# Each head's columns of the compressed keys and values projected once, and the exchanged copy written by VectorE

## The reference, cut to what matters

```
k_c, v_c = columns of u @ w_in            # (256 tokens, 2 groups x 64) each
chunks = t.reshape(b, g, seq // 16, 16, 64)
blocks = concat([chunks[:, :, m:m + 15] for m in range(2)], axis=3) + pos_emb
flat   = blocks.reshape(b, g, 15, 32 * 64)
return gelu(flat @ w1 + b1) @ w2 + b2
```

## Time and profile before

| | |
|---|---|
| median of 3 runs | 1196.41 us (1195.58 to 1196.82) |
| the profiled execution | 1196.96 us, of which the span in the trace is 1194.9 us |
| PE busy | 1084.8 us, 91% of the span |
| DVE, ACT, POOL busy | 472.8, 412.7, 194.1 us |
| moved by DMA | 333.58 MB |

### The profile page before, as it was taken

The page is one execution under the profiler, slowest core; times in us unless marked ns, Lnnn a source line. Parts: engine busy times, 40 slices in busy tenths (PEclk is TensorE's granted clock), DMA queues, the critical chain, the costliest instruction groups (busy, mean ns, idle before and its releaser), DMA issues. The chain is left out here.

```text
span 1194.9 us, 17411 instructions
## 1 busy us (share of the span) xinstructions
PE 1084.8 (91%) x6862; PEld 706.2 (59%) x6862; DVE 472.8 (40%) x1046; ACT 412.7 (35%) x790; POOL 194.1 (16%) x272
## 2 busy tenths in 40 slices
PE   8999888999888988788888899878999899999997
PEld 7887545567422424344544235346887686999775
DVE  4566456435200001123333011106747546444655
ACT  5445453342110001104332002004436454444873
POOL 1002552000000000003120000004432223001550
PEclk9999999999999999999999999999999999999999
DMA  9657599826799999999999999995531203666300
GB/s 363 235 171 262 217 345 311 311 97 281 307 429 427 422 423 411 430 397 416 419 427 422 422 422 415 425 418 189 180 127 54 89 28 117 226 184 187 107 20 35
DMA packets 55720, 333.58 MB, mean 279 GB/s; under 512 B 5840, under 2 KB 6096, under 8 KB 43216
## 3 DMA queue, kind: packets, MB, share of 16 engines
q1 hardware_dynamic: 55632, 332.39, 71.6%
HBM read 331.32 MB, written 1.05 MB: 278 GB/s over the span
## 5 line engine op out<-in xcount | busy, mean ns | idle before, releaser
L486 ACT ACTIVATE ab<-w 128x1024 fp32r<-128x1024 f32 (+2 forms) x117 | 122.0, 1049 | 174.9 <-PE ps L502 171.1
L496 DVE TENSOR_TENSOR ab<-w,ab 128x1024 fp32r<-128x1024 f32 (+2 forms) x101 | 123.6, 1229 | 131.4 <-ACT ab L486 130.9
L2577 PE MATMUL ps<-w,vT 128*32 128x512 f32 x1024 | 126.6, 617 | 44.3 <-DMA w<-in_w_gate 28.5
L502 PE MATMUL ps<-ab,uA 128*128 128x512 f32 x320 | 101.3, 398 | 3.1 <-ACT gr L1591 1.3
L2577 PEld LDWEIGHTS ps<-w,vT 128*32 128x32 f32 x1024 | 28.7, 110 | 124.1 <-issue 76.0
L502 PE MATMUL ps<-UA,ab 128*128 128x256 f32 x512 | 93.8, 284 | 2.8 <-ACT h L1591 1.5
L502 PE MATMUL ps<-ab,UA 128*128 128x512 f32 (+1 forms) x288 | 87.9, 386 | 0.0
L502 PEld LDWEIGHTS ps<-UA,ab 128*128 128x128 f32 x512 | 80.2, 192 | 3.5 <-issue 1.7
L2625 PE MATMUL ps<-w,bT 128*32 128x512 f32 x512 | 63.0, 617 | 15.3 <-DMA w<-in_w_down 9.8
L502 PE MATMUL ps<-UB,ab 128*128 128x256 f32 x256 | 72.4, 283 | 0.0
L502 PEld LDWEIGHTS ps<-ab,uA 128*128 128x128 f32 x320 | 59.8, 190 | 17.8 <-issue 3.8
(11 more groups left out here) (554 smaller groups left out, 1883.4 us busy)
## 6 DMA issues: line engine op xcount, KB each, us to landing
w<-in_w_gate SPq DMA_DIRECT2D x32, 2048.0 KB, 13.4
w<-in_w_up SPq DMA_DIRECT2D x32, 2048.0 KB, 13.1
w<-in_w_down SPq DMA_DIRECT2D x32, 2048.0 KB, 13.4
w<-in_w_ada SPq DMA_DIRECT2D x48, 512.0 KB, 7.8
w<-in_w_c SPq DMA_DIRECT2D x42, 512.0 KB, 4.5
w<-in_w_m SPq DMA_DIRECT2D x16, 512.0 KB, 6.0
w<-in_ab_out_w SPq DMA_DIRECT2D x10, 512.0 KB, 4.7
w<-in_w_out SPq DMA_DIRECT2D x8, 512.0 KB, 9.4
```

The lines of the kernel that those rows point to most:

```text
L486: e.activation(sp.a(j), w.v, ACT.Copy).then_inc(sp.whole, 1)
L496: e.tensor_tensor(sp.b(j), w.v, sp.a(j).bitcast(F32), ALU.subtract).then_inc(sp.parts[j % NAB], 1)
L502: ins = e.matmul(out_, l[x], r[y], start=start and n == 0, stop=stop and n == 2)
L2577: ins = e.matmul(t.ps[o, :], ve[:, p % 2, 2 * c + k, o], w.v[:, 2 * a + k, :], start=c + k == 0, stop=c + k == 4)
```

## The change

The array `w_kvc` has 256 columns in place of 512: keys of group 0 and 1, values of group 0 and 1, each once. Its two tiles (kvc.0 and kvc.1) hold four of the eight contraction steps each, where four tiles held two. PE fills two banks, one for keys and one for values, with group 0 on partitions 0 to 63 and group 1 on 64 to 127. For each bank DVE now writes three pieces into `bS`: the bank as it is, its lower half into the upper partitions of a second place, and its upper half into the lower partitions. Then it makes all eight additions, reading from the first place where group and parity agree with the partitions, and from the second where they don't.

```diff
-        for n in ("gqk", "gv", "q", "kv", "kvc", "gr", "cq", "kva", "qa", "za", "zb"):
+        for n in ("gqk", "gv", "q", "kv", "gr", "cq", "kva", "qa", "za", "zb"):
...
+            if c < 2:
+                source[f"kvc.{c}"] = d["w_kvc"][:, 4 * c:4 * c + 4, :]
...
-            pe_linT(e, S1, "kvc", uA, uB)
+            two = [bank.take(ALL, "kvc") for _ in range(2)]
+            for c in range(2):
+                j = S1.add(f"kvc.{c}")
+                a, b = S1.a(j), S1.b(j)
+                S1.ready(e, j)
+                for m, t in enumerate(two):
+                    if c == 0:
+                        free(e, t)
+                    for k in range(4):
+                        o, n = slice(m * 128, m * 128 + 128), 4 * c + k
+                        ins = three(e, t.ps[:, 0:256], (a[:, k, o], b[:, k, o]), (uA[:, n, :], uB[:, n, :]), n == 0, n == 7)
...
-            act_lin(e, S1, "kvc", [])
+            act_splits(e, S1, "kvc.1", 3)
...
-            dve_lin(e, S1, "kvc")
+            rest_splits(e, "dve", S1, "kvc.1", 3)
             e.wait_ge(cleared, 1)
-            for j, t in enumerate(bank["kvc"]):
-                m, g = j // 2, j % 2
+            for m, t in enumerate(bank["kvc"]):
...
-                e.tensor_tensor(bS[:, 0, 0:256], t.ps[:, 0:256], rsrow[:, :], ALU.mult).then_inc(t.evac, 1)
+                e.tensor_tensor(bS[:, 0, 0:256], t.ps[:, 0:256], rsrow[:, :], ALU.mult)
+                e.tensor_tensor(bS[64:128, 1, 0:256], t.ps[0:64, 0:256], rsrow[0:64, :], ALU.mult)
+                e.tensor_tensor(bS[0:64, 1, 0:256], t.ps[64:128, 0:256], rsrow[64:128, :], ALU.mult).then_inc(t.evac, 1)
...
+                for g in range(2):
+                    for jp in range(2):
+                        p0 = 64 * jp
+                        src = bS[p0:p0 + 64, g ^ jp, 0:256].rearrange("p (n s) -> p s n", s=16)
...
-                if j < 3:
+                if m == 0:
                     V_.did(ins)
+                    rest_splits(e, "dve", S1, "gr.3")
...
-        "w_kvc": tiles(w_in, 8, *[half(col[m], g) for m in (1, 2) for g in (0, 0, 1, 1)]),
+        "w_kvc": tiles(w_in, 8, *[half(col[m], g) for m in (1, 2) for g in range(2)]),
```

More of the change, by code:

```diff
@@ L1457, in pe_first @@
             pe_lin(e, S1, "kv", uA, uB, 512, range(2))
-            pe_linT(e, S1, "kvc", uA, uB)
+            two = [bank.take(ALL, "kvc") for _ in range(2)]
[9 more added lines that the diff above has]
+                        ins = three(e, t.ps[:, 0:256], (a[:, k, o], b[:, k, o]), (uA[:, n, :], uB[:, n, :]), n == 0, n == 7)
+                    if c == 1:
+                        ins.then_inc(t.full, 1)
+                if c == 0:
+                    S1.gone(j, ins)
+                else:
+                    S1.done[j] = (t.full, t.n)
             pe_lin(e, S1, "gr", uA, uB, 512, range(2))
@@ L1784, in dve_first @@
                 V_.after()
-                e.tensor_tensor(bS[:, 0, 0:256], t.ps[:, 0:256], rsrow[:, :], ALU.mult).then_inc(t.evac, 1)
+                e.tensor_tensor(bS[:, 0, 0:256], t.ps[:, 0:256], rsrow[:, :], ALU.mult)
+                e.tensor_tensor(bS[64:128, 1, 0:256], t.ps[0:64, 0:256], rsrow[0:64, :], ALU.mult)
+                e.tensor_tensor(bS[0:64, 1, 0:256], t.ps[64:128, 0:256], rsrow[64:128, :], ALU.mult).then_inc(t.evac, 1)
                 e.wait_ge(t.evac, t.n)
[L1787 to L1792, removed]
-                if j < 3:
+                for g in range(2):
+                    for jp in range(2):
+                        p0 = 64 * jp
+                        src = bS[p0:p0 + 64, g ^ jp, 0:256].rearrange("p (n s) -> p s n", s=16)
+                        for half in range(2):
+                            ins = e.tensor_tensor(Bt[p0:p0 + 64, m, 8 * half:8 * half + 8, 15 * g:15 * g + 15], src[:, jp:16:2, half:half + 15],
+                                                  bc(pos[p0:p0 + 64, 8 * half:8 * half + 8], 2, 15), ALU.add)
+                if m == 0:
                     V_.did(ins)
+                    rest_splits(e, "dve", S1, "gr.3")
                 else:
                     ins.then_inc(cmp_rows, 1)
-                if j == 1:
-                    rest_splits(e, "dve", S1, "gr.3")
             dve_lin(e, S1, "gr")
```

## The result

| | before | after |
|---|---|---|
| median of the runs, us | 1196.58 (1194.3 to 1197.9) | 1190.43 (1186.85 to 1192.48) |
| profiled execution, us | 1196.96 | 1191.98 |
| its span, us | 1194.9 | 1190.2 |
| PE busy, us | 1084.8 | 1079.1 |
| granted clock, mean | 0.986 | 0.986 |

The ratio is 0.9948, with a 95% interval of [0.9929, 0.9967]: 6.2 us, between 3.9 and 8.5. The forecast was 1189.1, range 1187.3 to 1192.3. The time is right to 1.3 us, and the way to it is half right. The experiments show that the gain is that of the removed matmuls. Of the 1.5 us that the sum adds to them, 1.3 rest on a fall of the clock that one execution of the kernel before had and another had not.

A forecast was written before the change was run, and what follows sets the result against it. The prediction took PE to bound the projections and transfers the experts. Its terms, 5.76 + 1.87 - 0.32 = 7.3 us, gave a forecast of 1189.1 us, with 1187.3 to 1192.3 for 8 in 10.

The forecast's parts named there:

- What it removes on PE: In kvc, 48 matmuls of 256 columns in place of 96, at 120 ns each: 5.76 us less.
- What it adds on DVE: For the kvc banks, 0.42 us per exchanging piece, 3.90 us a bank; DVE 0.57 us later against gr's start.
- m00.0 and m00.3: At m00: start 12.7 us after gr's start (T), last quarter waiting 0.7 us for DVE's split; gain against T 1.87 us.
- The clock: In m00: no clock fall expected behind a pause cut from 1.34 to 0.58 us; m00 took 12.72 us, gr 11.0.
- Rival 1: Behind la, the clock falls all the same and m00 takes its 12.72 us: gain 6.5 us, 1189.9; chance 0.17.
- m10.2: At m10.2, PE waits 0.3 us for POOL's split, leaving 1.5 us of gain against gr's start.
- Does it reach the end?: From 130 us on, the experts included, the same timeline 7.3 us earlier, since DMA queues are almost empty there.
- the turned banks: In the first GLA product, the second half no longer shares bank 4 with an unread result: at most 0.3 us, left out.
- the sign of being wrong: Late gr.3 (pause at 75 us), exchanging piece over 0.7 us, or shift of 7 us at 130 and less at 300.
- Rival 2: DVE costs more, 1.23 us per exchanging piece, or gain is handed back behind: 4.1 us gain, 1192.3; chance 0.13.
- rival 3: Transfers take the gain back, the experts' stream being anchored by something unmoved: nothing remains, 1196.4; chance 0.07.
- rival 4: Slower: exchanging pieces on DVE from 2.25 us each eat the whole gain, at 3.1 us each 1199.8; chance 0.03.

The follow-up runs named there:

- e8: The changed kernel with each kvc step done twice into its bank, 96 matmuls as before; 1196.95 us, ratio to before 1.0005.
- e5: The kernel before with the two early expert tiles issued at a later step, behind w_out; 1195.71 us, ratio to before 0.9991.
- e3: The changed kernel with the two early expert tiles issued at a later step, behind w_out; 1189.45 us, ratio to before 0.9934.
- e1: The changed kernel with the ring of PSUM banks turned back by two behind la; 1190.99 us, ratio to before 0.9945.
- e9: The changed kernel with the two early expert tiles issued later and the bank ring turned by two only ahead of out; 1189.50 us, ratio to before 0.9940.
- e0: The changed kernel run once more, unedited; 1190.29 us, ratio to before 0.9943.
- e7: The changed kernel without the exchanging pieces, results wrong for half the groups, for its times alone; 1189.17 us, ratio to before 0.9946.
- e2: The changed kernel with the bank ring skipping two between kvc and gr, so gr and m00 use their former banks; 1193.03 us, ratio to before 0.9957.
- e11: The changed kernel with early expert tiles issued later, the bank ring turned by two ahead of out, and the exchange on POOL; 1187.19 us, ratio to before 0.9932.

## Why the prediction was right, and where it was not

*What it removes on PE.* Right: 5.75 us for 5.76, in every trace with 48 matmuls. e8 shows that the gain in time hangs on it: with these matmuls put back, the rest of the change is worth between 1.4 us of gain and 2.6 of loss.

*What it adds on DVE.* Right: 0.42 a piece, 3.92 a bank for 3.90. DVE came to the three splits 0.73 us later against T, and to m00.3's 0.86 and not 0.57 later; the small differences lie in the starts, by 0.1 at a time.

*m00.0 and m00.3.* The places, releasers and starts are right (T + 12.82 for 12.7, a wait of 0.59 for 0.7). Their worth was not. Against the trace of before the gain is 26.18 - 24.82 = 1.36 us for 1.87: m00 starts 0.1 later than forecast, and its matmuls take 11.41 us without the wait, where the sum has 10.9. Against e5, where the clock holds before as well, it is 0.06: the earlier start gains 0.64 us, and the later split takes it back, m00 ending at T + 24.88 before and T + 24.82 after.

*The clock.* This is the step that failed. The sum sets m00's 12.72 us against gr's 11.0 and so has the fall at 1.72, as a cost of the kernel before. By e5 it is 1.30, and it is chance: 12.72 us for m00 in one execution, 11.42 in another of the same code behind the same pause. Rival 1's last sentences named it: the Trainium skill ("TensorE: Matmul & The Clock Gate", part 1) has a transition fall elsewhere from run to run. The runs here agree and go further, since here a fall can stay away altogether: behind pauses of 1.34 us (three times) and 1.89 the clock fell twice and held twice. I gave that sentence no consequence for the sum, where it has one. A forecast that is set against a median may count such a fall only as often as it comes, which in three traces nobody can tell. The term is worth between nothing and 1.3 us, not the whole, and the forecast should have been up to 1.3 us higher.

*m10.2.* The 0.3 us of waiting fell away, but not since POOL was early: it began its split at T + 34.18 (102.02), 0.2 later than forecast, and had half of it at T + 36.54. PE came for it 0.5 later than forecast, at T + 36.59, because m00 had ended 0.5 later. So the shift there, 7.07 us, is 5.75 + 1.36 - 0.04.

*Does it reach the end?* The claim that all behind 130 us moves by the same amount holds to 218 us and fails there. Two gaps that were just closed before opened: w_out behind 4 MB of early expert tiles, and bank 4. The prediction looked at whether the queues were empty at 130 us and not at what each later landing stood behind; and it set the turned banks at a gain of 0.3 us at most, which is what they are worth at m11 (0.40), while they cost 0.87 at routing. e3, e1 and e9 show both causes by removing them. This is the sign of being wrong that the prediction named itself: a shift that is 7 us at 130 and less at 300.

*The end.* The 4.6 us that are missing at routing are not missing in the medians, which are 6.2 to 6.8 under before. Two things can be shown. Up to the experts' first w_down a shift is handed on exactly where the clock holds: in the nine runs with a granted clock of 1.00 from 280 to 290 us, first w_down and routing are earlier by the same amount, to 0.07 us. In the four where it fell there, 1.6 to 3.3 us of the shift are gone by then (e0 3.3, e3 3.3, e7 1.6, e2 1.7), three of them behind the wait for bank 4 and e2 without it. And the experts' stage hands on a shift only roughly. From the issue of the first w_down to the end of the span, fourteen traces have 883.1 to 888.2 us, without an order by kernel: 886.6 before, 884.1 and 884.4 in the two traces of the changed one. In that stage the DMA share is 0.98 to 1.00, and the mean granted clock of an execution goes with its time: over the 29 runs of before in the second session at about -0.7 us for each 0.001 of clock (correlation -0.65), in the other two sessions at -0.6 and -0.4 (-0.74 and -0.55). A pause that costs 2 us in one trace is below what that leaves visible. Whether the changed kernel truly wins back time in the experts, or its two traces were poor ones at routing, stays open; e9 and e11, with both repairs, are 1 and 3 us under it in the medians, which is the size to expect and is within the intervals.

*The rivals.* Rival 1's time, 1189.9, is the nearest to the median; its mechanism did not occur, though the size at m00 is what remains when the chance is taken out. Rival 2's price for a piece was wrong, but that DVE's time counts one to one is as it says. Of rival 3 a part came true, at the context's transposes, though by another stream: w_out's tiles, and not the experts', came less early than PE did. Nothing spoke for rival 4.

So the number is right for its largest term, 5.75 us of matmuls, and for the rest by luck. Both errors lean the same way, towards too much gain: 1.3 us that hang on chance, and losses behind 225 us that the prediction did not have, 4.2 us between m10.2 and routing in the trace. That the time is off by 1.3 us only is because the medians show little of these losses, and why they don't is open.

## What to carry to other kernels

Before a stall in one trace goes into a sum, ask whether the same code shows it in a second execution; behind pauses of 1.34 to 1.89 us ahead of m00 the clock fell in two of four traces here. When work is taken out early, everything behind that was ready "just in time" must be looked up one by one: the landing that a reader has no idle time for, and what stands ahead of it in the queue. And a change in the number of buffers taken from a rotating ring turns all later uses of it: list which unread result each later stage now meets.

## What the runs showed of the hardware

- DVE reads one half of the partitions in PSUM and writes the other at no extra cost: 0.42 us for 64 x 256, as within a half.
- POOL copies 64 x 256 crosswise in SBUF in some 0.45 us each (two in 0.90 and 0.98), while DVE's additions beside it, in another order, took 2.62 us for eight, against 2.57 without POOL's copies.
- Behind a pause before the context's transposes the clock fell in the three traces with 1.97, 2.14 and 2.24 us, and in none of the five with 0.60, 1.29, 1.56, 1.80 and 1.90; behind la it fell twice and held once at 1.34, and held at 1.89. Behind the 0.87 us at routing it fell in three of seven traces (e0, e3, e7). The length of the pause alone doesn't tell.
- Times of one and the same kernel spread over up to 11.5 us in a session. The mean granted clock accounts for some three to six tenths of the variance of before (the squares of 0.55, 0.65 and 0.74), and what accounts for the rest stays open.
